# A one-core transformer kernel: the inverse inside the delta rule, from two 64-row chunks side by side to block-diagonal 128-row tiles, and its steps in another order

## The reference, cut to what matters

```python
decay = jnp.exp(jnp.where(incl, gcum[..., :, None] - gcum[..., None, :], -jnp.inf))
kb = kc * bc[..., None]
a_mat = jnp.where(strict, jnp.einsum('nbhid,nbhjd->nbhij', kb, kc) * decay, 0.0) \
    + jnp.eye(c, dtype=jnp.float32)
rhs = jnp.concatenate([vc * bc[..., None], kb * jnp.exp(gcum)[..., None]], axis=-1)
sol = lax.linalg.triangular_solve(a_mat, rhs, left_side=True, lower=True, unit_diagonal=True)
u_val, k_cum = sol[..., :dv], sol[..., dv:]
```

## Time and profile before

| | |
|---|---|
| median of 3 runs | 1098.03 us |
| the profiled execution | 1098.61 us |
| its span, first to last instruction | 1096.9 us |
| granted TensorE clock, mean | 0.997 |
| TensorE busy | 99% of the span |
| VectorE busy | 70% |
| ScalarE busy | 54% |
| GpSimd busy | 3% |
| DMA, mean over the span | 168 GB/s of HBM reads |

### The profile page before, as it was taken

How to read it: one execution, slowest core, us unless ns; L and a number is a source line. 1 busy time by engine, 2 the same in 40 slices (tenths; PEclk the granted TensorE clock), 3 DMA queues, 4 the chain that set the end, 5 groups by cost and what they waited for, 6 DMA issues and landing times.

```text
span 1096.9 us, 16775 instructions
## 1 busy us (share of the span) xinstructions
PE 1081.5 (99%) x7038; PEld 949.7 (87%) x7038; DVE 765.2 (70%) x907; ACT 588.2 (54%) x731; POOL 36.9 (3%) x93
## 2 busy tenths in 40 slices
PE   9999999999999999999998999999999999999997
PEld 8899999999988888888897888888898888888886
DVE  5587888564769998886676676556578676656564
ACT  6467754336466656556655544444464766444443
POOL 6000000000000000000006000000000000000000
PEclk9999999999999999999999999999999999999999
DMA  8453433333555555555442555555544344555551
GB/s 315 158 188 116 154 128 142 117 117 123 185 183 179 190 191 192 193 192 188 172 154 85 186 192 192 192 192 192 192 134 155 135 154 167 191 188 192 189 187 58
DMA packets 27453, 185.03 MB, mean 169 GB/s; under 512 B 3169, under 2 KB 3681, under 8 KB 5618
## 3 DMA queue, kind: packets, MB, share of 16 engines
q1 hardware_dynamic: 26208, 182.46, 47.7%
q10 hardware_dynamic: 1170, 1.49, 0.4%
HBM read 182.89 MB, written 1.05 MB: 168 GB/s over the span
## 4 chain that ended last, share of the span: by engine, by line
PE 94%; DVE 3%; ACT 1%; issue 1%; DMA 0%; DVEq 0%; ACTq 0%
PE ps L2044 17%; PE ps L2114 12%; PE ps L2129 12%; PE ps L2116 12%; PE ps L2050 9%; PE ps L2082 7%; PE ps L2088 7%; PE ps L2083 7%; PE ps L2149 1%; PE ps L2064 1%; DVE low L1349 1%; PE ps L2465 1%; PE ps L2219 1%; PE ps L2317 1%; PE ps L2328 0%
## 5 line engine op out<-in xcount | busy, mean ns | idle before, releaser
L915 ACT ACTIVATE whi<-raw 128x2048 fp32r<-128x2048 f32 x170 | 324.4, 1913 | 274.9 <-PE ps L2129 132.7
L1349 DVE TENSOR_TENSOR low<-raw,whi 128x2048 fp32r<-128x2048 f32 x170 | 389.4, 2293 | 34.8 <-ACT whi L915 31.8
L2044 PE MATMUL ps<-hboth,whi 128*128 128x512 f32 x864 | 216.7, 392 | 1.2 <-DVE conv L1797 1.2
L2044 PEld LDWEIGHTS ps<-hboth,whi 128*128 128x128 f32 x864 | 157.2, 188 | 31.9 <-issue 2.5
L2114 PE MATMUL ps<-whi,ahi 128*128 128x512 f32 x416 | 163.7, 393 | 0.0
L2116 PE MATMUL ps<-whi,alo 128*128 128x512 f32 x416 | 162.7, 391 | 0.0
L2082 PE MATMUL ps<-hboth,whi 128*128 128x256 f32 x544 | 137.4, 291 | 0.0
L2083 PE MATMUL ps<-hboth,whi 128*128 128x256 f32 x544 | 133.1, 283 | 0.0
L2050 PEld LDWEIGHTS ps<-hboth,low 128*128 128x128 f32 x864 | 117.9, 190 | 8.5
L2050 PE MATMUL ps<-hboth,low 128*128 128x256 f32 x864 | 120.5, 282 | 0.0
L2129 PE MATMUL ps<-low,ahi 128*128 128x512 f32 x416 | 119.7, 389 | 0.0
(11 more groups left out here) (380 smaller groups left out, 1226.4 us busy)
## 6 DMA issues: line engine op xcount, KB each, us to landing
raw<-in_ffn_up SPq DMA_DIRECT2D x32, 1024.0 KB, 4.8
raw<-in_ffn_down SPq DMA_DIRECT2D x32, 1024.0 KB, 4.9
raw<-in_w_up SPq DMA_DIRECT2D x22, 1024.0 KB, 4.8
raw<-in_w_gate SPq DMA_DIRECT2D x12, 1024.0 KB, 4.9
raw<-in_w_down SPq DMA_DIRECT2D x11, 1024.0 KB, 4.9
raw<-in_w_dn SPq DMA_DIRECT2D x6, 1024.0 KB, 5.0
raw<-in_w_sc SPq DMA_DIRECT2D x6, 1024.0 KB, 4.8
raw<-in_w_branch SPq DMA_DIRECT2D x6, 1024.0 KB, 4.8
```

Source lines behind the costliest of these rows:

```text
L915: act.activation(whi[:, u % SPLIT, :], raw[:, u % RAW, :], ACT.Copy).then_inc(sem("hi_done"), 1)
L1349: dve.tensor_tensor(wlo[:, u % RAW, :], raw[:, u % RAW, :], whi[:, u % SPLIT, :].bitcast(F32), ALU.subtract).then_inc(sem("lo_done"), 1)
L2044: pe.matmul(out, whi[:, s, at:at + P], hboth[:, k, :, :].rearrange("p a t -> p (a t)"), start=k == 0, stop=False, skip_group_check=True)
```

## The change

- `Bl`, `LT` and `Y` are full: 128 partitions x 4 heads x 128 columns. `LT` holds the whole matrix of the tile, with the block between the chunks, and `Loff` goes. `Bl` is `LT` masked with the full `lev[l]`. `Y` lies in `xs`, is zeroed once for each tile (in `dn_pre`) and is then written in its two diagonal blocks only, by two ScalarE instructions instead of one. X and XT stay packed (64 columns).
- `dn_kk` multiplies keys by keys in 4 full matmuls instead of 8 + 4 of 64 columns, and VectorE has one operation of 128x512 where there were three and two on narrower parts.
- `dn_y` and the second half of `dn_z` (Y^T XT) are 4 matmuls with a full 128x128 stationary tile and 64 moving columns each. The first half of `dn_z` stays 64x64, and so do `dn_off` and `dn_join`.
- The masking of L for the next level (`dn_between`) is done by VectorE behind `dn_z` of the level before, no longer in a `dn_y` of its own.
- `steps_at`: before, y and z of both tiles stand close together in 8 slots from 51 to 59, with slot 55 empty; after, each slot from 51 to 60 has the z of one tile and a y or dn_off of the other. `dn_x0` of tile 0 moves from slot 50 to 49; the end (`dn_off`, `dn_join`, `dn_sol`) of tile 0 or both comes one slot later, `dn_state` 0 shares slot 63 with `dn_sol` 1, and `dn_new` stays in 64.
- `lev` moves in the arena from 13312 to 17280, so `fox_gates` waits on VectorE for GpSimd's constants.

```diff
--- before.py
+++ after.py
@@ -329,19 +329,21 @@
         47: [("dn_kk", 1)],
-        50: [("dn_x0", 0), ("dn_x0", 1)],
-        51: [("dn_y", 0, 1), ("dn_y", 1, 1), ("dn_z", 0, 1), ("dn_z", 1, 1)],
-        52: [("dn_y", 0, 2)],
-        53: [("dn_y", 1, 2), ("dn_z", 0, 2), ("dn_z", 1, 2)],
-        54: [("dn_y", 0, 3), ("dn_y", 1, 3), ("dn_z", 0, 3), ("dn_z", 1, 3)],
-        56: [("dn_y", 0, 4)],
-        57: [("dn_y", 1, 4), ("dn_z", 0, 4), ("dn_z", 1, 4)],
-        58: [("dn_y", 0, 5), ("dn_y", 1, 5), ("dn_z", 0, 5)],
-        59: [("dn_z", 1, 5), ("dn_off", 0)],
-        60: [("dn_off", 1), ("dn_join", 0)],
-        61: [("dn_join", 1), ("dn_sol", 0)],
-        62: [("dn_sol", 1)],
-        63: [("dn_state", 0)],
+        49: [("dn_x0", 0)],
+        50: [("dn_x0", 1), ("dn_y", 0, 1)],
+        51: [("dn_z", 0, 1), ("dn_y", 1, 1)],
+        52: [("dn_z", 1, 1), ("dn_y", 0, 2)],
+        53: [("dn_z", 0, 2), ("dn_y", 1, 2)],
+        54: [("dn_z", 1, 2), ("dn_y", 0, 3)],
+        55: [("dn_z", 0, 3), ("dn_y", 1, 3)],
+        56: [("dn_z", 1, 3), ("dn_y", 0, 4)],
+        57: [("dn_z", 0, 4), ("dn_y", 1, 4)],
+        58: [("dn_z", 1, 4), ("dn_y", 0, 5)],
+        59: [("dn_z", 0, 5), ("dn_y", 1, 5)],
+        60: [("dn_z", 1, 5), ("dn_off", 0)],
+        61: [("dn_off", 1), ("dn_join", 0)],
+        62: [("dn_join", 1), ("dn_sol", 0)],
+        63: [("dn_state", 0), ("dn_sol", 1)],
@@ -674,15 +676,15 @@
 
-        X, XT, LT, Bl = [[packed(a_, k), packed(b_, k)] for a_, b_, k in
-                         ((own_[0], tops[0], 0), (own_[1], tops[1], 0), (own_[1], tops[1], 1), (flat[0], tops[2], 0))]
-        Y = [packed(flat[1], 0), packed(tops[2], 1)]
-        Loff = [packed(own_[0], 1), packed(tops[0], 1)]
+        X, XT = [[packed(own_[0], k), packed(tops[0], k)] for k in range(2)]
+        LT = [by(own_[1], DH), by(tops[1], DH)]
+        Bl = [by(flat[0], DH), by(tops[2], DH)]
+        Y = [by(xs[:, 0, 512 * t:512 * t + 512], DH) for t in range(TT)]
         DT = [by(flat[0], DH), by(tops[3], DH)]
         reach = [by(own_[0], DH), by(tops[0], DH)]
         XF = [by(own_[2], DH), by(own_[3], DH)]
         dnout = by(tops[3], DH)
-        lev = view(13312, 6 * P).rearrange("p (l j) -> p l j", l=6)
+        lev = view(17280, 6 * P).rearrange("p (l j) -> p l j", l=6)
@@ -1072,11 +1074,14 @@
                 act.wait_ge(sem("dn_BX"), 2 * (l - 1) + t + 1)
-                act.activation(Y[t], packed(ps[:, 7 - t, :], 0), ACT.Copy).then_inc(sem("dn_Y"), 1)
+                for c_ in chunks:
+                    ins = act.activation(Y[t][c_, :, c_], packed(ps[c_, 7 - t, :], 0), ACT.Copy)
+                ins.then_inc(sem("dn_Y"), 1)
 
             def dn_off(t):
                 act.wait_ge(sem("dn_off"), t + 1)
-                act.activation(Y[t][chunks[1]], packed(ps[chunks[1], 7 - t, :], 0), ACT.Copy).then_inc(sem("dn_Yoff"), 1)
+                second = chunks[1]
+                act.activation(Y[t][second, :, second], packed(ps[second, 7 - t, :], 0), ACT.Copy).then_inc(sem("dn_Yoff"), 1)
@@ -1481,6 +1486,7 @@
             def fox_gates():
+                dve.wait_ge(sem("constants"), made["delta"])
@@ -1637,6 +1643,7 @@
                                   wide(rk[:, :, t].unsqueeze(2), [DH, P]), ALU.mult)
+                dve.memset(Y[t], 0.0)
@@ -1651,16 +1658,10 @@
                 dve.wait_ge(sem("dn_kked"), 2 * t + 1)
-                first, second = chunks
-                kk = ps[:, kk_banks[t][0], :]
-                for c_ in chunks:
-                    dve.tensor_tensor(LT[t][c_], packed(kk[c_], 0), DT[t][c_, :, c_], ALU.mult)
-                link(dve.tensor_tensor(Loff[t][first], packed(kk[first], 1), DT[t][first, :, second], ALU.mult))
+                link(dve.tensor_tensor(LT[t], by(ps[:, kk_banks[t][0], :], DH), DT[t], ALU.mult))
                 dve.wait_ge(sem("dn_kked"), 2 * t + 2)
-                link(dve.tensor_tensor(qkT[:, t], by(ps[:, kk_banks[t][1], :], DH), DT[t], ALU.mult))
-                dve.tensor_tensor(LT[t], LT[t], wide(bk[:, t, :].unsqueeze(2), [DH, CH]), ALU.mult)
-                ins = dve.tensor_tensor(Loff[t][first], Loff[t][first],
-                                        bk[first, t, :].unsqueeze(2).to_broadcast([CH, DH, CH]), ALU.mult)
+                dve.tensor_tensor(qkT[:, t], by(ps[:, kk_banks[t][1], :], DH), DT[t], ALU.mult)
+                ins = dve.tensor_tensor(LT[t], LT[t], wide(bk[:, t, :].unsqueeze(2), [DH, P]), ALU.mult)
@@ -1669,13 +1670,17 @@
                     dve.wait_ge(sem("constants"), made["all"])
-                link(dve.tensor_tensor(Bl[t], LT[t], wide(levp[:, 0, :].unsqueeze(1), [DH, CH]), ALU.mult))
-                dve.tensor_tensor(XT[t], wide(idp.unsqueeze(1), [DH, CH]), Bl[t], ALU.subtract)\
+                for c_ in chunks:
+                    ins = dve.tensor_tensor(XT[t][c_], LT[t][c_, :, c_], levp[c_, 0, :].unsqueeze(1).to_broadcast([CH, DH, CH]),
+                                            ALU.mult)
+                link(ins)
+                dve.tensor_tensor(XT[t], wide(idp.unsqueeze(1), [DH, CH]), XT[t], ALU.subtract)\
                    .then_inc(sem("dn_x0"), 1)
                 dve.wait_ge(sem("dn_x0"), t + 1)
-
-            def dn_y(t, l):
-                dve.tensor_tensor(Bl[t], LT[t], wide(levp[:, l, :].unsqueeze(1), [DH, CH]), ALU.mult)\
+                dn_between(t, 1)
+
+            def dn_between(t, l):
+                dve.tensor_tensor(Bl[t], LT[t], wide(lev[:, l, :].unsqueeze(1), [DH, P]), ALU.mult)\
@@ -1688,6 +1693,7 @@
                     own(dve.tensor_tensor(XT[t], XT[t], packed(ps[:, 2 * t, :], 0), ALU.subtract), "dn_X2", 2 * n_)
+                    dn_between(t, l + 1)
@@ -2283,14 +2289,8 @@
                 k_, q_ = dnT[:, DH:2 * DH, t * P:(t + 1) * P], dnT[:, 0:DH, t * P:(t + 1) * P]
-                first, second = chunks
                 for h in range(DH):
-                    for c_ in chunks:
-                        pe.matmul(ps[c_, kk_banks[t][0], h * CH:(h + 1) * CH], k_[:, h, c_], k_[:, h, c_],
-                                  start=True, stop=True)
-                for h in range(DH):
-                    ins = pe.matmul(ps[first, kk_banks[t][0], (DH + h) * CH:(DH + h + 1) * CH], k_[:, h, first],
-                                    k_[:, h, second], start=True, stop=True)
+                    ins = pe.matmul(ps[:, kk_banks[t][0], h * P:(h + 1) * P], k_[:, h, :], k_[:, h, :], start=True, stop=True)
@@ -2313,9 +2313,7 @@
                 for h in range(DH):
-                    for c_ in chunks:
-                        ins = pe.matmul(ps[c_, 7 - t, h * CH:(h + 1) * CH], Bl[t][c_, h, :], X[t][c_, h, :],
-                                        start=True, stop=True)
+                    ins = pe.matmul(ps[:, 7 - t, h * CH:(h + 1) * CH], Bl[t][:, h, :], X[t][:, h, :], start=True, stop=True)
@@ -2325,20 +2323,18 @@
                     for c_ in chunks[0:1] if l == LEVELS - 1 else chunks:
-                        ins = pe.matmul(ps[c_, 2 * t + 1, h * CH:(h + 1) * CH], XT[t][c_, h, :], Y[t][c_, h, :],
+                        ins = pe.matmul(ps[c_, 2 * t + 1, h * CH:(h + 1) * CH], XT[t][c_, h, :], Y[t][c_, h, c_],
                                         start=True, stop=True)
                 ins.then_inc(sem("dn_XBX"), 1)
                 for h in range(DH):
-                    for c_ in chunks:
-                        ins = pe.matmul(ps[c_, 2 * t, h * CH:(h + 1) * CH], Y[t][c_, h, :], XT[t][c_, h, :],
-                                        start=True, stop=True)
+                    ins = pe.matmul(ps[:, 2 * t, h * CH:(h + 1) * CH], Y[t][:, h, :], XT[t][:, h, :], start=True, stop=True)
                 ins.then_inc(sem("dn_XBX"), 1)
 
             def dn_off(t):
                 first, second = chunks
                 pe.wait_ge(sem("dn_X2"), 4 * (LEVELS - 2) + 2 * t + 1)
                 for h in range(DH):
-                    ins = pe.matmul(ps[second, 7 - t, h * CH:(h + 1) * CH], Loff[t][first, h, :], X[t][first, h, :],
+                    ins = pe.matmul(ps[second, 7 - t, h * CH:(h + 1) * CH], LT[t][first, h, second], X[t][first, h, :],
@@ -2347,7 +2343,7 @@
                 for h in range(DH):
-                    ins = pe.matmul(ps[first, 2 * t + 1, h * CH:(h + 1) * CH], Y[t][second, h, :], XF[t][second, h, second],
+                    ins = pe.matmul(ps[first, 2 * t + 1, h * CH:(h + 1) * CH], Y[t][second, h, second], XF[t][second, h, second],
```

More of the change, by code:

```diff
@@ L1974, in _ @@
                          fox_out=fox_out, dn_unit=dn_unit, small_split=small_split, dn_cum=dn_cum, dn_tok=dn_tok,
-                         dn_pre=dn_pre, dn_decay=dn_decay, dn_kk=dn_kk, dn_x0=dn_x0, dn_y=dn_y, dn_z=dn_z, dn_sol=dn_sol,
+                         dn_pre=dn_pre, dn_decay=dn_decay, dn_kk=dn_kk, dn_x0=dn_x0, dn_z=dn_z, dn_sol=dn_sol,
                          dn_join=dn_join,
```

## The result

The changed kernel takes 1107.74 us (median of 4 runs, 1107.38 to 1108.21); the kernel before 1098.72 (4 runs, 1098.02 to 1100.93; with the three of the section on its time among them). The ratio is 1.0081 with a 95% interval of 1.0069 to 1.0094: 0.8% slower, and the medians lie 9.0 us apart. 1107.6 was predicted, 9.6 above the 1098.03 of the kernel before's first three runs. The profiled execution took 1108.0 (1108.2 was the sum), its span is 1106.3 against 1096.9.

What follows compares the result with a forecast made beforehand. TensorE, busy 99% of the span, was taken to bound the kernel. 7.5 + 1.0 + 1.1 + 0.2 + 0.2 - 0.5 - 0.8 + 0.9 = +9.6 us on 1098.03 gave 1107.6 us; range 1104.0 (leaving out A) to 1111.0.

Steps and rivals of the forecast that it cites:

- (1): Full products: ten y go from 0.47 to 0.81, ten second halves of z from 0.47 to 0.88; together +7.5 us.
- (2): Changes of tile: four more ways in and out +1.0, change inside z +1.1, three slow first records +0.2 us.
- (3): Slot 59: z's last group and off can no longer overlap; +0.2 us taken, bound 0 to 0.4.
- (4): Slots 51, 54 and 58: TensorE's 0.16 us wait for ScalarE's copy of Y goes; -0.5 us.
- Rival B: More waits: Y's copies queue on ScalarE, z waits some 0.5 us in about six of ten slots; +3, 1110.6 us; 10%.
- (5): dn_kk: keys and query products take 1.69 us instead of 2.08, no change of tile; -0.39 twice, -0.8 us.
- (6): dn_x0 of tile 0 in slot 49: TensorE waits for VectorE's chain; +0.9 us, bounds 0 and 1.4.
- (7): Taken as free: VectorE's larger between products, Y's memsets, fox_gates' wait, the later end of the solve, SyncE's loads.
- Rival A: Not slower: full tile's weights load behind the previous matmul, so records cost their moving columns; 1100.1 or 1099.2 us; 6%.
- The forecast's own upper bound: 1109.4 us, from groups of 0.91, a dn_x0 wait of 1.4 and an off loss of 0.4.

Runs made afterwards that it cites:

- moving_128: The changed kernel with 128 instead of 64 moving columns in six of eight records of y and z's second half; 1107.96 us in one run.
- keys_only: The kernel before with only the product of keys changed to 4 full matmuls; ratio 0.9996 (0.9988 to 1.0005), stage 0.55 us shorter.
- x0_in_50: The changed kernel with dn_x0 of tile 0 back in slot 50; 1106.87 us (4 runs), stage 1.02 us shorter.
- tiles_128x64: The changed kernel with y and z's second half as 8 matmuls of 128 rows and 64 weight columns each; 1101.62 us in one run.
- full_tiles_old_order: The changed kernel with the kernel before's steps_at; 1107.0 us (4 runs), ratio 1.0070 to the kernel before.

## Why the prediction was right, by its steps

**(1) and (2), the products and the changes of tile:** right in size. A slot of z and y by the prediction is 0.09 + 0.52 + 0.10 + 0.98 + 0.81 = 2.50; measured 2.51. Inside it two terms are off and cancel, which is luck: y takes 0.87, not the 0.81 of a group with 128 columns in front of a product, and z's full group 0.94 with the change of tile in it, not 0.98. Why y takes 0.87 stays open; it isn't the smaller number of columns, since moving_128 has the same 0.87 with 128 columns in six of eight records. A slip without weight: two more products have a slow first record, not three (18 in the stage for 16). That the price of a form that no row showed could be had from a one-column row and a 128-column row is confirmed by moving_128: both ends bound by the same thing, the weights.

**(3), the overlap of z and off:** right. In the kernel before slot 59 takes 1.45 from 232.40 (231.44 + 0.96) to 233.85, and its three groups one behind the other would be 0.09 + 0.52 + 0.47 + 0.57 = 1.65: an overlap of 0.20. After, slot 60 (z, off) takes 2.33 from 243.79 (242.83 + 0.96) to 246.12, where the prediction's terms give 2.40 without any overlap. First the kernel before, then the changed one:

```profile
231.44 1.12 PE L2088 MATMUL ps<-hboth,low 128*128 128x256 f32 x8
...
233.85 0.39 PE L2082 MATMUL ps<-hboth,whi 128*128 128x256 f32 x1
```

```profile
242.83 1.12 PE L2094 MATMUL ps<-hboth,low 128*128 128x256 f32 x8
...
245.52 0.67 PE L2337 MATMUL ps<-arena 64*64 64x64 f32 x8
246.12 0.39 PE L2088 MATMUL ps<-hboth,whi 128*128 128x256 f32 x1
```

**(4), no wait for Y:** right, and mis-sized. Before, z starts 0.65 behind the second y and its own first group takes 0.51 instead of 0.47 (193.91, 194.56, 195.07 in the earlier trace rows), so a wait costs 0.22 and three of them 0.66; the prediction has 0.5. The 0.05 by which its sum for slot 51 falls short (3.22 for 3.27) is this. ScalarE's two copies take 0.77 and are done long before z needs them (192.63 for 194.68); in answer to the earlier trace rows:

```profile
191.86 0.77 ACT L1078 ACTIVATE xs<-ps 64x256 f32<-64x256 f32 x2 [0.64 <-PE ps L2316]
197.33 0.77 ACT L1078 ACTIVATE xs<-ps 64x256 f32<-64x256 f32 x2 [4.70 <-PE ps L2316]
198.13 1.92 ACT L917 ACTIVATE whi<-raw 128x2048 fp32r<-128x2048 f32 x1
```

The split comes behind the copy, as the order has it. Rival B falls.

**(5), the keys:** right, -0.75 for -0.8. From 177.99 to 179.69 is 1.70, in answer to the earlier trace rows:

```profile
177.99 1.05 PE L2293 MATMUL ps<-arena 128*128 128x128 f32 x8
178.88 1.06 PE L2296 MATMUL ps<-arena 128*128 128x128 f32 x8
179.69 0.36 PE L2088 MATMUL ps<-hboth,whi 128*128 128x256 f32 x1
```

In the changed kernel the keys' gain comes whole, because VectorE's shorter dn_kk gives `dn_lt` earlier (177.2) than in keys_only. I had not seen that these two halves of the edit need each other.

**(6), the wait at dn_x0:** right in place, cause and size. VectorE's chain, in answer to the earlier trace rows, then TensorE:

```profile
175.23 0.69 DVE L1661 TENSOR_TENSOR arena<-ps,cy 128x512 f32<-128x512 f32 x1
...
182.86 2.29 DVE L1354 TENSOR_TENSOR low<-raw,whi 128x2048 fp32r<-128x2048 f32 x1
185.07 0.85 DVE L1674 TENSOR_TENSOR arena<-arena,packs 64x256 f32<-64x256 f32 x2
185.95 0.42 DVE L1677 TENSOR_TENSOR arena<-packs,arena 128x256 f32<-128x256 f32 x1
```

```profile
184.57 1.12 PE L2094 MATMUL ps<-hboth,low 128*128 128x256 f32 x8
186.43 0.68 PE L2305 MATMUL ps<-packs,arena 64*64 64x64 f32 x16 [0.74 <-DVE arena L1677]
```

The split starts at 182.86 (182.9 in the prediction), dn_x0 at 185.07 (185.1), and TensorE at 186.43 (186.5) instead of 185.62: 0.81 for 0.9. x0_in_50 takes it away and gains 1.02 with the change of tile that goes with it.

**(7), at nothing:** right; no other wait is new, and the rest of the kernel keeps its 840.5 us.

**Rival A** (weights hidden) falls by the 0.87 of the slots and by the two runs on the tile's form. The rule that the Trainium skill, "TensorEngine Tiling (Array Packing)", Instruction Overhead, states (one free column lasts as long as 60, some 60 cycles) fits these f32 groups only in that few columns save little: 0.106 us a record with one, 0.109 with 64 and with 128. As a size it does not: 60 cycles at 2.4 GHz are 0.025 us, an estimate from that page. Another rule of the same notes does: the Trainium skill, "TensorE: Matmul & The Clock Gate", LDWEIGHTS (loading the stationary operand), says that the load takes a time that goes with the columns and not with the rows, columns / 1.2 in ns. 107 ns for 128 and 53 for 64 columns by that page; the traces agree to a few per cent and to a tenth: 0.109 for 128 columns in moving_128, and 0.058 for 64 in one half alone (slot 47 before), with 64 rows as with 128: `dn_off`'s 8 records on 64 rows take 0.60 with both changes of tile in it (245.52 to 246.12 in the changed kernel). In tiles_128x64 two halves side by side take 0.032 a record, the change of tile included.

Sum: +9.6 predicted, +9.41 in the profiled stage. Term by term the stage has +9.8 for (1) and (2) together (what the others leave, and what was predicted), +0.2 for (3), -0.66 for (4), -0.75 for (5) and +0.81 for (6). The medians of the runs lie 9.0 apart, and the interval of the ratio allows 7.6 to 10.3. That the median of 1107.74 stands within 0.2 us of the predicted 1107.6 is in part luck: the sum was set on 1098.03, and the kernel before has 1098.72 with its fourth run. The forecast's own upper bound was added up 0.2 too low (groups of 0.91 are +1.3, the wait +0.5, off +0.2: 1109.6); it touches nothing, since rival B set the upper end.

## What to carry to other kernels

Count a small f32 matmul by the weight columns that load one after the other, not by its flops or by the number of instructions. Eight 64x64 products in two diagonal quarters, made into four full 128x128 ones, halve the instructions and nearly double the time (0.47 to 0.87): no fewer columns are loaded, and no two halves load side by side any more. Four full ones pay where they replace twelve products of 64 columns (the keys), since four of these had nothing to run beside them, and two changes of tile go too: in slot 47 the keys go from 1.17 us with the changes in it to 0.89, and the query products behind them from 0.91 to 0.81. When TensorE sets the end, sum its stream by distances between starts and then follow the other engines' chains only to the points where the new order lets TensorE arrive earlier than before; that is where the one new wait was.

## What the runs showed of the hardware that I had not expected

**The start of the kernel has two speeds.** In two profiles, x0_in_50 and full_tiles_old_order, dn_decay began at 170.84 and 170.93, in all others between 168.66 and 169.32, though the code of the kernel's start is the same. It is the first transposing products (x by a diagonal). In x0_in_50, then in the changed kernel:

```profile
7.73 5.43 PE L2169 MATMUL ps<-cy,xres 128*128 128x128 f32 x32 [1.84 <-POOL arena L833]
```

```profile
7.06 3.81 PE L2170 MATMUL ps<-cy,xres 128*128 128x128 f32 x32 [1.44 <-DVE cy L1369]
```

And the busy times of 7 to 13 us (PE, PEld, DVE, ACT, POOL, then the granted clock, the DMA share and GB/s), x0_in_50 first:

```profile
7.00:10.00 3.00, 2.27 (x13) 2.30 (x14) 2.37 (x5) 1.97 (x5) 2.60 (x7) 0.73 1.04 399
10.00:13.00 3.00, 3.00 (x22) 3.00 (x20) 0.30 (x1) 1.18 (x3) 2.29 (x12) 0.70 1.05 436
```

```profile
7.00:10.00 3.00, 2.94 (x26) 2.97 (x27) 1.79 (x4) 2.29 (x6) 2.55 (x8) 1.00 1.03 391
10.00:13.00 3.00, 2.87 (x16) 1.89 (x16) 2.75 (x7) 3.00 (x9) 2.47 (x9) 1.00 1.04 433
```

The granted clock is 0.73 and 0.70 there, part of the time at the lower level of 1.2 GHz, against 1.00 at 2.4 GHz. Ahead of it TensorE stood idle for 1.84 us (1.94 in the other slow start); x had come 0.2 to 0.3 us later and VectorE's product of the diagonal took 0.7 us instead of 0.3. In the changed kernel it stood idle for 1.44. A late x alone is not enough: tiles_128x64 starts these products just as late, at 7.71, after 1.70 us of idle, and its granted clock is 1.00. From their first start to the first product they take 5.19 us (to 12.92) against 3.56 (to 10.62), so it costs 1.6 us beside the late x, as much as the new order did with full tiles, and it differs between executions of kernels whose starts are the same (x0_in_50's profiled execution took 1108.41, its other three 1106.32 to 1106.90). Why the clock fell in these two stays open. I did not try an edit that keeps TensorE busy there.

**The part behind the stage scatters too**, 839.65 to 840.89 us in ten profiles, with no order that I could tie to an edit. Its cause stays open.
